# Page rows issued by GpSimd, page numbers by one register load, and a rotated attention loop in a one-core decoder step

## What is computed

```python
# prompt, causal                                   # sample, over gathered pages
s = (einsum('bqhr,bkr->bhqk', q_abs, kv_c)         past_c  = cache_kv_latent[l, page_table]   # (8, 2048, 256)
   + einsum('bqhd,bkd->bhqk', q_pe, k_pe)) * SCALE past_pe = cache_k_rope[l, page_table]      # (8, 2048, 64)
p = softmax(where(causal, s, -inf))                s = concat([q . past, q . new]) * SCALE
o = einsum('bhqk,bkr->bqhr', p, kv_c)              o = softmax(s)[:, past] @ past_c + ... @ kv_c
```

## Time and profile before

| | us |
|---|---|
| median of 3 runs | 2664.46 (2657.72 to 2664.70) |
| profiled execution, its own time | 2664.49 |
| its span | 2662.6 |
| PE busy | 2474.7 (93%) |
| DVE, ACT, POOL busy | 923.2, 604.7, 918.9 |
| attention loop | about 483 to 718 us of the span |

### The profile page before, as it was taken

How to read it: one execution, slowest core, us unless ns; L and a number is a source line. 1 busy time by engine, 2 the same in 40 slices (tenths; PEclk the granted TensorE clock), 3 DMA queues, 4 the chain that set the end, 5 groups by cost and what they waited for, 6 DMA issues and landing times.

```text
span 2662.6 us, 47816 instructions
## 1 busy us (share of the span) xinstructions
PE 2474.7 (93%) x19003; PEld 2390.1 (90%) x19003; DVE 923.2 (35%) x1245; ACT 604.7 (23%) x830; POOL 918.9 (35%) x380
## 2 busy tenths in 40 slices
PE   7999878767799988999999999999999999999996
PEld 7999867444589987999999999999999999999996
DVE  6200497555543356621221221221221221311266
ACT  5111432121221142321121221221211211211211
POOL 2443442100034431333333333333333333333342
PEclk9999989778899999999999999999999999999998
DMA  5222232456342232222222222222222222222222
GB/s 226 88 87 87 95 131 72 148 160 212 111 173 90 89 119 112 77 87 86 87 86 86 86 87 88 86 86 86 86 88 86 87 87 87 86 87 87 87 84 90
DMA packets 96252, 270.75 MB, mean 102 GB/s; under 512 B 11761, under 2 KB 44562, under 8 KB 94930
## 3 DMA queue, kind: packets, MB, share of 16 engines
q1 hardware_dynamic: 92448, 251.96, 28.6%
q10 hardware_dynamic: 3762, 18.21, 1.8%
HBM read 263.79 MB, written 6.33 MB: 101 GB/s over the span
## 4 chain that ended last, share of the span: by engine, by line
PE 68%; issue 23%; POOL 5%; DVE 3%; ACT 0%; POOLq 0%; DVEq 0%
PE psum L1212 67%; POOL hl L357 5%; DVE square L1048 1%; DVE square_sum L1050 1%; DVE x L1045 0%; DVE x L1199 0%; PE psum L1242 0%; DVE head_max L1085 0%; PE psum L1542 0%; PE psum L1519 0%; PE psum L1576 0%; PE psum L1561 0%; DVE rstd_x L715 0%; ACT mem_probs L615 0%; PE psum L1531 0%
## 5 line engine op out<-in xcount | busy, mean ns | idle before, releaser
L357 POOL TENSOR_TENSOR hl<-raw,hl 128x1024 fp32r<-128x1024 f32 x376 | 918.7, 2444 | 1711.6 <-ACT hl L660 933.0
L1212 PE MATMUL psum<-xg,hl 128*128 128x272 f32 x10272 | 1305.8, 290 | 31.7 <-DVE xg L710 20.2
L1212 PEld LDWEIGHTS psum<-xg,hl 128*128 128x128 f32 x10272 | 1301.7, 190 | 34.4 <-POOL hl L357 21.3
L1212 PE MATMUL psum<-ffn_hidden,hl 128*128 128x272 f32 x6144 | 776.1, 288 | 0.0
L1212 PEld LDWEIGHTS psum<-ffn_hidden,hl 128*128 128x128 f32 x6144 | 775.3, 188 | 0.0
L660 ACT CAST hl<-raw 128x1024 fp32r<-128x1024 f32 x254 | 266.3, 1048 | 1230.8 <-PE psum L1212 1230.8
L1187 DVE TENSOR_TENSOR x<-x,psum 128x544 f32 x112 | 80.8, 722 | 570.2 <-PE psum L1212 570.2
L1172 DVE SCALAR_TENSOR_TENSOR square<-psum,rstd_x 128x544 f32<-128x544 f32 x64 | 46.4, 725 | 500.5 <-PE psum L1212 500.5
L1176 DVE TENSOR_SCALAR ffn_hidden<-square 128x544 f32 x64 | 132.4, 2069 | 60.7 <-ACT square L669 60.7
L386 ACT CAST hl<-raw 128x1024 fp32r<-128x1024 f32 x64 | 67.1, 1048 | 314.7 <-PE psum L1212 314.7
L379 ACT CAST hl<-raw 128x1024 fp32r<-128x1024 f32 x58 | 60.4, 1045 | 185.9 <-PE psum L1212 132.3
(11 more groups left out here) (234 smaller groups left out, 1201.0 us busy)
## 6 DMA issues: line engine op xcount, KB each, us to landing
raw<-in_w_stream SPq DMA_DIRECT2D x376, 512.0 KB, 3.3
page_cols<-in_pool_t SPq DMA_DIRECT2D x128, 192.0 KB, 3.6
page_rows<-in_pool_n SPq DMA_DIRECT2D x128, 128.0 KB, 3.0
x<-in_x_t ACTq DMA_DIRECT2D x4, 1088.0 KB, 12.3
out<-x SPq DMA_DIRECT2D x8, 544.0 KB, 2.8
cache_k_sb<-in_mem_k_t SPq DMA_DIRECT2D x1, 4096.0 KB, 13.6
cache_v_sb<-in_mem_v_p SPq DMA_DIRECT2D x1, 4096.0 KB, 23.0
x<-in_x_t ACTq DMA_DIRECT2D x1, 4080.0 KB, 14.0
```

Source lines behind the costliest of these rows:

```text
L357: nc.gpsimd.tensor_tensor(HL[s % 2][:, 1, :, :], RAW[:, s, :, :], HL[s % 2][:, 0, :, :].bitcast(F32), ALU.subtract).then_inc(w_lo, 1)
L1212: last = mm(PSUM[:, s + half, 0:HALF], HL[slot][:, wp, blk, :], src[:, xp, k, HALF * half:HALF * (half + 1)], start=start and n == 0, stop ...
```

## The change

It has five parts.

1. SP no longer issues the page rows. POOL does, in its own loop over the samples, placed between the low parts of weight units 73 and 74.
2. Both SP and POOL read the 16 page numbers of a sample with a single load into 16 registers.
3. The loop is rotated. The first page scores and maxima stand ahead of it; inside a turn the next head's scores come right after this head's values, and the next sample's page scores before the sample's last transposes. The seventh and eighth turn are written out behind the loop, the eighth without preparing a ninth.
4. The rotary query is put on both halves of the 128 partitions, and the rotary key is held with its high part on one half and its low part on the other (`PEH` shrinks from two planes to one), so that a rotary score takes two products instead of three. DVE makes the extra copies, in a staging step that is split in two: `stage_q` ahead of the probabilities, `stage_k` behind them.
5. Smaller: the sample's sum goes to another PSUM place, the square of a head's result to another buffer.

```diff
@@ sync @@
-                pages_of = [sp.value_load(PTAB[0:1, bass.ds(b * PAGES + g, 1)], min_val=0,
-                                          max_val=pool_n.shape[0] - 1) for g in range(PAGES)]
+                _, pages_of = nc.values_load_multi_w_load_instructions(
+                    PTAB[0:1, bass.ds(b * PAGES, PAGES)], engines=[mybir.EngineType.SP], min_val=0,
+                    max_val=pool_n.shape[0] - 1)
...
-                sp.wait_ge(pvs, b + 1)
-                for g in range(PAGES):
-                    sp.dma_start(NAT[:, g, :], pool_n[bass.ds(pages_of[g], 1), :, :]
-                                 .rearrange("a p n -> (a p) n")).then_inc(ld_nat, 16)
@@ gpsimd @@
+            with pool.Fori(0, NB) as b:
+                _, pages_of = nc.values_load_multi_w_load_instructions(
+                    PTAB[0:1, bass.ds(b * PAGES, PAGES)], engines=[mybir.EngineType.Pool], min_val=0,
+                    max_val=pool_n.shape[0] - 1)
+                pool.wait_ge(pvs, b + 1)
+                for g in range(PAGES):
+                    pool.dma_start(NAT[:, g, :], pool_n[bass.ds(pages_of[g], 1), :, :]
+                                   .rearrange("a p n -> (a p) n")).then_inc(ld_nat, 16)
@@ vector, one turn @@
+                dve.wait_ge(s_top, h + 1)
+                step(nc.vector.reduce_max(SM[:, :], PSUM[:, 5, NS:NS + 4], AX))
+                ts(SB[:, :], SM[:, :], -MLA_SCALE, None, ALU.mult).then_inc(s_bias, 1)
+                if not last:
+                    stage_q(nxt, pair, 1 - hp, step)
...
+                done.then_inc(pn, 1)
+                if not last:
+                    stage_k(nxt, step)
+                    stage_sample(nxt)
@@ tensor, rotary scores @@
-                    for n3, (qp, kp) in enumerate(PASSES):
-                        last = mm(PSUM[:, qb, 0:w], QRH[rows, qp, 128 * qb:128 * qb + 128], PEH[rows, kp, 0:w],
-                                  start=False, stop=n3 == 2)
+                    for part in range(2):
+                        last = mm(PSUM[:, qb, 0:w], QRH[:, part, 128 * qb:128 * qb + 128], PEH[:, 0:w], start=False,
+                                  stop=part == 1)
```

More of the change, by code:

```diff
@@ L525, in _ @@
             act.wait_ge(c_n, 8)
[L526 to L549, removed]
@@ new lines, in head_exp, with sample_exp @@
+            def head_exp(h):
+                act.wait_ge(nb, h + 1)
+                for qb in range(4):
+                    n = (qb + 1) * 128
+                    last = nc.scalar.activation(PR[:, P_AT[qb]:P_AT[qb] + n], PSUM[:, qb, 0:n], ACT.Exp,
+                                                bias=HN[:, qb:qb + 1], scale=MLA_SCALE,
+                                                accum_out=HS[:, qb:qb + 1])
+                last.then_inc(ex, 1)
+            def sample_exp(b):
+                act.wait_ge(s_bias, b + 1)
+                nc.scalar.activation(S[:, :], PSUM[:, 4, :], ACT.Exp, bias=SB[:, :], scale=MLA_SCALE,
+                                     accum_out=SS[:, 0:1])
+                nc.scalar.activation(PNW[:, :], SNW[:, :], ACT.Exp, bias=SB[0:NS, :], scale=MLA_SCALE,
+                                     accum_out=SS[0:NS, 1:2]).then_inc(sex, 1)
@@ new lines, in attend_turn @@
+            def attend_turn(i, hp, last):
+                h = i * 2 + hp
+                for kb in range(4):
+                    w = NP - 128 * kb
+                    act.wait_ge(pt, h * 4 + (kb + 1))
+                    lo = 0 if kb < 3 else 128
+                    nc.scalar.copy(PTH[kb][:, 0, lo:lo + w], PSUM[:, kb, 128 * kb:NP]).then_inc(pt_hi, 1)
+                act.wait_ge(s_t, h + 1)
+                nc.scalar.copy(PST[:, :, :], PSUM[:, 5, :].rearrange("p (g q) -> p g q", g=QUART))
+                nc.scalar.copy(PNT[0:NS, :], PSUM[0:NS, 7, 256:256 + NS]).then_inc(pst, 1)
+                if not last:
+                    head_exp(h + 1)
+                    sample_exp(h + 1)
@@ L941, in _ @@
             stage_sample(0)
-            stage_v(0, step).then_inc(stg_v, 1)
+            stage_v(0, step)
             dve.wait_ge(w_lo, U_OUT + 4)
@@ new lines, in page_scores @@
+            def page_scores(b):
+                pe.wait_ge(qst, b + 1)
+                pe.wait_ge(pst, b + 1)
+                for q in range(4):
+                    pe.wait_ge(ld_kt[q], (b + 1) * (16 * QUART))
+                for r in range(RT):
+                    for q in range(4):
+                        mm(PSUM[NS * q:NS * q + NS, 4, :], QA[:, r, :], KT[q][:, :, 128 * r:128 * r + 128],
+                           start=r == 0, stop=False)
+                for q in range(4):
+                    last = mm(PSUM[NS * q:NS * q + NS, 4, :], QR[:, :], KT[q][:, :, 256:384], start=False, stop=True)
+                last.then_inc(kt_used, 1)
+                for r in range(RT):
+                    mm(PSUM[0:NS, 5, 0:NS], QA[:, r, :], KS[:, r, :], start=r == 0, stop=False)
+                mm(PSUM[0:NS, 5, 0:NS], QR[:, :], PES[:, :], start=False, stop=True).then_inc(sn, 1)
```

294 lines of the change are left out of this document (160 added, 134 removed).

## The result

The changed kernel takes 2617.49 us (median of four executions, 2616.21 to 2622.67), the kernel before 2664.58 us (four, 2657.72 to 2666.23): a ratio of 0.9832, interval 0.981 to 0.9853. I had forecast 2635.5 us, with a range of 2630 to 2642 for the forecast itself and of 2627 to 2664 with most of its rivals. The profiled execution took 2617.44 us with a span of 2615.7 us.

The account below looks back on a forecast made before the run. SP's issues and number loads were taken to bound the attention loop, then a PE and DVE chain. 2664.5 - 26.8 (seven turns) - 4.1 (last turn) + 1.9 (start) = 2635.5 us; own range 2630 to 2642, with most rivals 2627 to 2664.

Parts of the forecast that it names:

- The reference: Whole kernel: starting time for the forecast, profiled execution 2664.49 us against median 2664.46, taken without correction.
- Bound before, and what relieves it: Attention loop: SP's issues and number loads, 27.4 us per turn, set the pace; relief is worth the distance to the next limit.
- The turn, 23.8 us: Attention loop: ten steps sum to 23.6 us, plus 0.2 for colder starts; seven periods instead of 27.63 save 26.8 us.
- Step 2: Loop turn: next head's scores, 4.51 us instead of 5.41, the rotary half losing a third.
- Step 8: Loop turn: DVE's `stage_q`, three copies and three subtractions as before, 2.94 us.
- Step 1: Loop turn: transposes and values after the head's probabilities, 5.50 us with the hop.
- The ends: Around the loop: eighth turn saves 4.1 us; longer first staging and first turn lose 1.9 us together.
- Step 5: Loop turn: page scores to DVE's maximum, 2.84 us, with SP's columns issued early enough to be there.
- B: Rival, loop: POOL a little late, 1.16 to 1.4 us per issue, page rows bound the turn; 2647 or 2657 us; chance 0.18.
- C: Rival, loop: slower, POOL above 1.41 us per issue, perhaps blocked by DVE's copies; 2686 us at 1.6; chance 0.12.
- D: Rival, loop: no change, POOL's issues slow DVE's three `stage_q` subtractions; turn 27.7 us, time 2663; chance 0.07.
- F: Rival, loop: better, clock stays up over DVE's tail, transposes and values lose 0.7 us per turn; below 2630; chance 0.06.

Follow-up runs that it names:

- b_pool: Kernel before with the changed kernel's SP and GpSimd programs (page rows on GpSimd, one number load), loop not rotated; ratio 0.9963 to the kernel before.
- a_sp: Changed kernel with the page rows back on SP, number load still a single one; ratio 0.9948 to the kernel before.
- b_rope: Kernel before with only the stacked rotary halves, all else unchanged; ratio 1.0012 to the kernel before.
- a_group: Changed kernel with 64-row rotary products again, a head's twelve rotary products placed behind its twelve plain ones; ratio 0.9871 to the kernel before.
- a_norope: Changed kernel with 64-row rotary products again, three passes per group, alternating with plain ones; ratio 0.9863 to the kernel before.
- a_probs: Changed kernel with the staging taken off the chain, scalings ahead of the page maximum, ACT's sample exponentials later; ratio 0.9779 to the kernel before, median 2590.4 us.
- a_again: Changed kernel measured again, unaltered, on another occasion; ratio 0.9875 to the kernel before.
- a_third: Changed kernel measured a third time, unaltered, on another occasion; ratio 0.9872 to the kernel before.

## Why the prediction was wrong where it was

*The reference.* This is the step that failed: "Profiled execution 2664.49 (the median is 2664.46, so no correction)", and an own range made of turns alone. It took the 1945 us behind the loop for a constant. It isn't one, and it came out 17.0 us shorter: the profiled execution of before had the widest of the four spacings seen (124.44, 125.00, 125.56 and 126.11 ns), and that of after the closest, 20.5 us apart over the FFN. That the one execution had the wide spacing and the other the close one is luck, as far as these runs can tell. With the medians over all occasions the gain is 33 us, 4 more than forecast. The trace of before held the hint: 806 products per 100 us ahead of the loop against 795 in the FFN, at the same granted clock.

*Bound before, and what relieves it.* Right. b_pool shows SP's cycle, a_sp that the page rows have to leave SP, b_rope that nothing else pays before that.

*The turn, 23.8 us.* Six full turns had 23.2 us on the mean, close, by errors that cancel in part. Step 2 was the largest: 3.23 us instead of 4.51. I wrote that three rotary products of 64 rows cost what three plain ones do, which is so in the earlier trace rows, because each group there pays one change of row count; a_group, a_norope and b_rope show the change, not the product, to be the price. Step 8 took 3.49 us (601.73 to 605.22) instead of 2.94. Its six instructions start 0.44 and 0.70 us apart where those of the turn I had read start 0.34 and 0.60 us apart. GpSimd's issues beside them are not the reason, for in a_sp, which has none, they are also 0.70 us apart; in b_pool the distance changes from head to head, 0.60 us in the turn at 584.53 and 0.70 us in that at 609.11. I had taken the duration from a head with the short one; the trace of before has 2.94 us in every second turn and about 3.35 us in the others. What makes the difference is open. Step 1 (transposes and values) had 5.8 us on the mean of six turns instead of 5.7. The seventh period was 19.99 us: the last turn stages nothing for a ninth head, which I counted for its scores and forgot for `stage_q`.

*The ends.* The start was too cheap, the tail too good. The loop began 5.6 us later, not 1.9. PE's first head scores came 2.6 us later: 1.5 us by the longer staging (I had 1.05), and 1.1 us because the staging itself began later, which no run explains. Then the first page columns landed 1.5 us more slowly, beside GpSimd's first rows, to which I had given nothing; and the staging behind the spread product took 1.0 us (I had 0.9). The tail saved 1.3 us instead of 4.1, by the 2.92 us wait for rows in the last turn. Loop +7.4, start -3.7, tail -2.8: the 29.9 us look like my 29.0 by luck as much as by mechanism.

*GpSimd.* An issue takes 0.58 to 0.6 us where I had estimated 1.0 and allowed 1.16, the number load about 5 us of an allowed 7.8. The 1 us that the Trainium skill gives (DMA: Bandwidth & Descriptors, section Specifications) is a time to the first byte and no issue time; no row shows a first byte, and the quickest of GpSimd's transfers landed whole after 2.2 us. Step 5's "some 4 to land" for SP's columns was up to 8.2 us beside GpSimd's rows; it cost nothing in the turn, since SP issues them nearly 20 us ahead of need. Rivals B and C fall, except that the stall behind the 113th transfer is B for one turn. C's rule (the Trainium skill, SBUF — State Buffer, section SBUF: two separate sides: a GpSimd transfer starves while VectorE copies) doesn't show: at 598.09 to 606.89 us fifteen transfers went out in 8.80 us beside DVE's copies at 601.73 to 603.06. Their landings do grow, from 2.4 to 6.1 us, but they begin to behind SP's first column at 599.55 us, 2 us ahead of the copies. Beside DVE's scalings and with no transfer of SP's in flight six row transfers of a_probs landed in 2.3 to 2.7 us, as quickly as any. No run has the copies beside GpSimd's transfers without SP's, so for the copies the rule isn't refuted; it is only not needed. D falls too: the subtractions took 0.69 us, as before. F was not the reason: the granted clock was still 0.50 from 585 to 587 us, under the transposes.

## What to carry to other kernels

Before a prediction of one per cent, compare the spacing of equal products in stages that the change doesn't touch, and give the rest of the program its own spread; three executions that agree don't bound it. When an issuing queue sets a loop's pace, relieve it first: the stacked halves were worth 2.7 us before that and 10.6 us after. On PE, keep products with equal row counts together, and then look for the consumer's idle gaps: moving the scalings into one, together with the rest of a_probs, took 24.7 us off the loop, the rotation 8.2.

## What was not expected of the hardware

Back-to-back products of 128x272 on a PE that never waits, at a granted clock of 1.00, have one of four mean spacings, 124.44, 125.00, 125.56 or 126.11 ns. Each held through the windows of a stage and may be another in the next stage or the next execution of the same program (a_again 124.44, a_third 125.56 ns), so nothing that is fixed in the program decides it alone. What draws it stays open.

A change between products of 128 and of 64 rows costs 0.19 us on the mean of six, and in a_norope's starts about as much in either direction.

GpSimd stood for 3.35 to 3.40 us behind its 113th transfer in after and in b_pool, at 667.90 and 676.33 us, though it was waiting for nothing that the trace shows. It did so in all ten traces with its transfers, 3.9 to 4.3 us from the start of the 113th to that of the 114th, where others are 0.58 us apart. What it does there is open. In b_pool:

```profile
675.79 0.54 POOL L368 DMA_DIRECT2D page_rows<-in_pool_n  x1 [16.86 <-PE psum L1476]
679.73 8.77 POOL L368 DMA_DIRECT2D page_rows<-in_pool_n  x15 [3.40 <-issue]
```

One load of sixteen page numbers took 4.75 us on GpSimd (537.10 to 541.85 us in after), and SP's gap with it is 5.75 us in a_sp, against 10.95 us with sixteen single ones.

Transfers issued by SP and by GpSimd at the same time slow each other: in the turn of the changed kernel from 597 us on GpSimd's take 2.4 to 6.1 us to landing and SP's up to 8.2 us, where SP's take 3.65 us on the median in a_sp, which has none of GpSimd's.
